# Two modulation units of a trunk step moved ahead of the second output projection, in between the group products

## The reference

```
m = silu(c) @ w_ada + b_ada;  shift, scale, gate = split(m, 3)     # 3 x 1024 values per sublayer
h = x * (1 + scale) + shift
x = layer_norm(ALPHA * x + (1 + gate) * sublayer(h))
```

```
pooled = causal means over windows 2, 4, 8, 16 (one per group of 256 channels) - h
mixed  = einsum('blgc,gcd->blgd', pooled, w_grp) * pool_scale      # 4 groups of 256 x 256
m      = mixed @ w_out
```

## Time and profile before

| | us |
|---|---|
| median of 3 runs (851.91 to 852.33) | 852.32 |
| the profiled execution's own time | 850.87 |
| its span | 849.0 |
| TensorE busy | 741.4 (87%) |
| ScalarE busy | 282.3 (33%) |
| VectorE busy | 240.7 (28%) |
| GpSimd busy | 130.0 (15%) |

### The profile page before, as it was taken

The page is one execution under the profiler, slowest core; times in us unless marked ns, Lnnn a source line. Parts: engine busy times, 40 slices in busy tenths (PEclk is TensorE's granted clock), DMA queues, the critical chain, the costliest instruction groups (busy, mean ns, idle before and its releaser), DMA issues.

```text
span 849.0 us, 22536 instructions
## 1 busy us (share of the span) xinstructions
PE 741.4 (87%) x9606; PEld 463.7 (55%) x9607; DVE 240.7 (28%) x596; ACT 282.3 (33%) x571; POOL 130.0 (15%) x217
## 2 busy tenths in 40 slices
PE   3799999899999999897886789978999979889964
PEld 2378887575655555453443368644555535545532
DVE  1139998714700000000000381272000000000033
ACT  2135677412433333322131250142333223323323
POOL 0170687400001001000000000001101101000101
PEclk9899999799999999999897889999999989999985
DMA  9999523995994989999999999697899999999301
GB/s 313 390 239 359 199 100 119 339 340 201 410 381 192 370 329 405 420 425 426 419 421 417 382 368 407 231 396 308 339 426 415 428 417 426 420 423 424 139 0 51
DMA packets 63885, 280.48 MB, mean 330 GB/s; under 512 B 3013, under 2 KB 3627, under 8 KB 55638
## 3 DMA queue, kind: packets, MB, share of 16 engines
q1 hardware_dynamic: 60738, 271.75, 81.2%
q0 software_dynamic: 2432, 6.94, 2.6%
q10 hardware_dynamic: 676, 1.24, 0.5%
HBM read 277.49 MB, written 3.37 MB: 331 GB/s over the span
## 4 chain that ended last, share of the span: by engine, by line
PE 62%; DMA 21%; DVE 7%; ACT 4%; SPq 2%; issue 2%; POOL 0%; DVEq 0%; ACTq 0%
PE bank L716 17%; DMA ring<-in_w_up 13%; PE bank L850 9%; PE bank L726 7%; PE bank L988 7%; PE bank L689 5%; PE bank L751 4%; DMA big<-in_w_up 4%; DMA ring<-in_w_ada 3%; PE bank L567 3%; DVE t L1353 2%; PE bank L697 2%; ACT big L1291 2%; DMA big<-in_state_pool 2%; SPq L474 1%
## 5 line engine op out<-in xcount | busy, mean ns | idle before, releaser
L716 PE MATMUL bank<-ring,big 128*32 128x256 f32 x2112 | 128.9, 399 | 25.8 <-DMA ring<-in_w_up 22.5
L716 PEld LDWEIGHTS bank<-ring,big 128*32 128x32 f32 x2112 | 70.8, 115 | 79.7 <-DMA ring<-in_w_up 21.1
L1918 POOL TENSOR_TENSOR big<-t 128x192 f32<-128x192 f32 x51 | 26.4, 518 | 547.9 <-PE bank L689 411.7
L1787 DVE SCALAR_TENSOR_TENSOR big<-big,bank 128x128 f32<-128x128 f32 x49 | 17.0, 347 | 307.8 <-ACT big L1289 307.8
L689 PE MATMUL bank<-htm,big 128*32 128x256 f32 x1224 | 75.5, 379 | 1.2 <-POOL big L1921 1.2
L850 PE MATMUL bank<-big,ring 128*128 128x264 f32 x320 | 73.9, 389 | 0.0
L716 PE MATMUL bank<-big 128*32 128x256 f32 x1024 | 63.0, 401 | 9.8 <-DMA big<-in_w_up 6.5
L850 PEld LDWEIGHTS bank<-big,ring 128*128 128x128 f32 x320 | 60.0, 190 | 11.5 <-issue 0.8
L726 PE MATMUL bank<-ring,big 128*32 128x256 f32 x1056 | 63.8, 382 | 0.0
L1289 ACT ACT_TABLE_LOAD x49 | 62.9, 1283 | 1.7 <-issue 0.8
L567 PE MATMUL bank<-ring,cT 128*32 128x256 f32 x768 | 53.6, 426 | 10.2 <-DMA ring<-in_w_ada 9.7
(11 more groups left out here) (252 smaller groups left out, 842.2 us busy)
## 6 DMA issues: line engine op xcount, KB each, us to landing
ring<-in_w_ada SPq DMA_DIRECT2D x24, 2048.0 KB, 18.4
ring<-in_w_gate SPq DMA_DIRECT2D x21, 2048.0 KB, 22.6
ring<-in_w_up SPq DMA_DIRECT2D x21, 2048.0 KB, 24.8
ring<-in_w_down SPq DMA_DIRECT2D x21, 2048.0 KB, 26.5
big<-in_w_gate SPq DMA_DIRECT2D x11, 2048.0 KB, 15.3
big<-in_w_up SPq DMA_DIRECT2D x11, 2048.0 KB, 18.8
big<-in_w_down SPq DMA_DIRECT2D x11, 2048.0 KB, 19.0
ring<-in_w_in_even SPq DMA_DIRECT2D x5, 2048.0 KB, 33.1
```

What stands on the lines that cost most here:

```text
L716: last = mm(GU[C * q:C * (q + 1), :].rearrange("p (a n) -> p a n", a=2), hgc[:, P * (k % 2) + C * (k // 2):P * (k % 2) + C * (k // 2 + 1)] ...
L1918: v.tensor_tensor(flat, all_r, all_b[:, :, bass.ds(g, 1)].broadcast_to([P, 2 * TT, C]), ALU.mult)\
```

## The change

On TensorE, unit 18 with the columns of 17 now stands behind the second group tile, and unit 19, without columns, behind the fourth. The projection has no unit left in it; behind its tiles 1 and 3 only the columns of 18 and of 19 stand. The call of `ada_columns` ahead of the projection is gone, and `ada_unit(20)`, which used to do the columns of 19, finds none pending. On ScalarE the copies of the two units' rows move in the same way between the copies of the group tiles. What is computed is the same.

```diff
@@ -990,8 +990,10 @@
                     last.then_inc(E(name + "_done"), 1)
                     if m == 5:
                         layer_norm_sum(idx, 0)
-                    if m in units:
+                    if units.get(m):
                         ada_unit(units[m])
+                    elif m in units:
+                        ada_columns()
                 layer_norm_sum(idx, 1)
@@ -1045,10 +1047,13 @@
                     last = mm(bank[4 + i % 4][:, 0:T], wgrp[:, g, c, P * hf:P * (hf + 1)], t1[:, 2 * g + c, :],
                               start=(c == 0), stop=(c == 1))
                 last.then_inc(E("grp_done"), 1)
-            ada_columns()
+                if i == 1:
+                    ada_unit(18)
+                if i == 3:
+                    ada_unit(19, False)
             pe.wait_ge(E("prow_copied"), 2)
             pe.wait_ge(E("grp_copied"), 5)
-            projection("out1", 2, t2, 4, lambda i: (E("grp_copied"), i + 1), GROUP_TILES, {3: 18, 5: 19})
+            projection("out1", 2, t2, 4, lambda i: (E("grp_copied"), i + 1), GROUP_TILES, {1: None, 3: None})
             layer_norm_mean(2)
             ada_unit(20)
@@ -1324,8 +1329,8 @@
                 act.wait_ge(E("grp_done"), i + 1)
                 A(fn(t2[:, m, :], bank[4 + i % 4][:, 0:T], ACT.Identity, scale=vec[:, V_PS + m:V_PS + m + 1]),
                   E("grp_copied"))
-            ada_unit(18)
-            ada_unit(19)
+                if i in (1, 3):
+                    ada_unit(18 + i // 2)
             warm_up(ACT.Sqrt)
             layer_norm(2, (20, 21))
             route(1, (22, 23))
```

## The result

The changed kernel takes 858.57 us (median of 7 runs, 855.35 to 859.96) against 852.32 (7 runs, 849.52 to 853.03). The ratio is 1.0065 with a 95% interval of 1.0047 to 1.0083, that is 5.5 us more, 4.0 to 7.1; the two medians by themselves differ by 6.25 us, which is inside that interval. Forecast were 858.1 us and +5.8 us.

What follows compares the result with a forecast made beforehand. Bounds: nearly saturated DMA engines, and TensorE without idle time up to the projection's end. Wait +4.96, lower clock +1.54, old wait -1.31, columns +0.46 and +0.09 gave 5.74 (5.77 step by step), so 858.1 us, range 855.4 to 860.8.

Steps and rivals of the forecast that it cites:

- The wait for unit 18's weights: Behind group tile 1, TensorE arrives at 504.32 and waits until the weights land at 509.28: 4.96 us.
- Unit 18 at the lower clock: After the idle wait, unit 18 takes 3.41 us instead of 1.87, +1.54 us.
- Unit 19 hardly waits, its landing is a floor: Behind group tile 3, TensorE arrives at 514.95, weights land at 514.84; an earlier arrival would wait for that landing.
- the second sum: End of the projection if unit 18 ran at full clock and TensorE waited for unit 19's landing: 5.66 us later.
- The old wait goes: In the group products, waiting and hand-over at VectorE's last pooled pair disappear under the new wait: -1.31 us.
- Columns of 19 win nothing behind the projection: Taking them out of unit 20 gains nothing, as TensorE waits there for ScalarE's squares; 0.46 us saved at most.
- Fills behind the projection's first tile: Layer 1 expert 0's fills go out about 8.8 us later, landing about 540, before use at 580.04 plus the shift: no loss.
- The sum: All terms together: the projection ends 5.77 us later, and what follows moves with it.
- The first (weights there, wait filled): Unit weights are ready in the group products, so the pooling wait is filled: 0.8 us earlier, 851.5 us; 5 in 100.
- The second (absorbed later): DMA waits in the expert loop absorb the later start: no change, 852.3 us; 5 in 100.
- The third (clock stays low): Low clock lasts past unit 18 into later tiles and unit 19: 859.6 us, at the outer end 865.0; 10 in 100.

Runs made afterwards that it cites:

- filled_wait: The changed kernel with ten products on constants ahead of unit 18, inside its wait; 858.10 us, +6.4 us against the kernel before.
- before_again: The kernel before, unchanged, profiled a second time; 34.17 us from the first group product to the last two projection tiles.
- weights_first: The changed kernel with the weight DMAs of units 18 and 19 issued ahead of the projection's two halves; 852.33 us, -0.3 us against the kernel before.
- late_in_groups: The changed kernel with unit 18 moved behind the sixth group tile and unit 19 behind the eighth; 854.69 us, +2.4 us against the kernel before.

## Why the prediction was right, step by step

- *The wait for unit 18's weights.* Forecast 4.96 us. The bracket shows 4.59, counted from the modelled end of the tile ahead; counted from start to start, as the sum does, it is 4.82 (511.08 - 504.46 - 1.80). By the formula it is landing minus arrival; the landing came 1.7 us later in the profile after (510.98 against 509.28), the arrival 1.94. The landings held against their issues, 21.7 and 20.4 us. What the forecast says of a DMA that is busy "nearly throughout" is too much (12 of the 40 slices of the earlier trace rows are below nine tenths), but the sum needs only the stretch of these transfers.
- *Unit 18 at the lower clock.* Forecast 3.41 us, measured 3.45 at a granted clock of 0.53.
- *Unit 19 hardly waits, its landing is a floor.* It started 0.4 us behind its landing. filled_wait turned the slow start into a wait for that landing; its stage is 5.02 us longer than the first of before, where the second sum said 5.66. Unit 19's weights landed 0.7 us earlier in it (494.32 + 20.3, that is 11.6 us behind the first group product instead of 12.3), which is the difference.
- *The old wait goes.* Right in the profile after. But its size, 1.31 us, was that of one execution. In before_again unit 16 and the products behind it ran at a granted clock of 0.50, unit 17 at 0.87, and from unit 16 to the group products were 7.97 us (495.39 to 503.36) instead of 6.54. TensorE reached the last tiles late enough, and there was no wait in the group products at all: they and the columns took 7.79 us, 0.22 more than their 7.57 of work, and the projection began at 511.15 against 511.40. The time that the lower clock cost ahead was given back here. So the term lies between 0.2 and 1.3 us, and the rival that lived on it (the wait filled, 0.8 us) was smaller than I made it.
- *Columns of 19 win nothing behind the projection.* From the norm's product (L606) to the second partial sum of squares (L599) were 4.04 us after (554.68 to 558.72), and 4.03 before (547.03 to 551.06); the columns that no longer stand between them made no difference:

```profile
554.68 0.71 PE L606 MATMUL bank<-ln_part,con 128*128 128x264 f32 x2 [0.51 <-ACT ln_part L1088]
555.33 1.93 PE L567 MATMUL bank<-ring,cT 128*32 128x256 f32 x32
...
558.72 0.65 PE L599 MATMUL bank<-big,con 128*32 128x264 f32 x8 [0.57 <-ACT big L1238]
```

- *Fills behind the projection's first tile.* Expert 0's first fill went out at 526.24, 11.0 us later than before, and landed in 8.2 us instead of 15.3. The queue had run nearly empty just ahead of it (DMA share 0.20 from 525.0 to 526.2), where it was full before (1.05 from 510 to 515):

```profile
526.24 0.34 SPq L474 DMA_DIRECT2D big<-in_w_gate  x1
big<-in_w_gate SPq DMA_DIRECT2D x1, 2048.0 KB, 8.2
525.00:526.20 1.20, 1.20 (x7) 1.04 (x6) 0.00 (x0) 0.00 (x0) 0.00 (x0) 1.00 0.20 79
```

  It was there at 534.4, more than fifty microseconds ahead of its use. Later, and harmless, as forecast; 8.8 us of delay had been forecast, and 1.94 of the 11.0 are the later start of the stage.
- *The sum.* + 5.77 forecast at the end of the projection, + 5.70 measured in the profile, + 5.5 (4.0 to 7.1) in time. Small errors cancel in it: the projection begins 18.02 us behind the first group product instead of 17.90, and the stage from there is 3.44 us shorter than before instead of 3.25, because a set of columns between its tiles costs 0.37 us, not 0.46. That the two sums agree within 0.1 us is in part luck, since the first profile of before happened to have the wait of 1.04 us: against the second the same sum, with 0.22 for 1.31, would have been + 6.9, and + 6.8 and + 6.5 were measured there. The interval in time holds all of these. The mechanism does not hang on it.

The rivals. The first (weights there, wait filled) is refuted by the bracket of 4.59 us; weights_first shows what it would have been worth, half a microsecond won against one profile of before and half a microsecond lost against the other. The second (absorbed later) is refuted by the chain: the fill behind the longest stall moved by 9.37 us with the product that releases it, and the loss is there in the time. The third (clock stays low) did not come: the tiles behind unit 18 took 1.95 us for eight passes (515.00 to 516.95; 1.88 before, 509.15 to 511.03), and unit 19 in 1.87 us. The Trainium skill's account of bursts between DMA waits (TensorE: Matmul & The Clock Gate, "HAM oscillation — how this bites in real kernels") holds here for the wait of 4.59 us and one slow start. In late_in_groups and filled_wait units stand behind waits of 0.75 to 1.23 us and start at the full clock, 1.86 to 1.87 us each (granted clock 1.00), so that not every wait between two bursts brings it.

## What to carry to other kernels

Before work is moved into an idle gap, look up when its inputs land, not only how long it takes: on an in-order engine the moved work turns the gap into a wait for them, and everything queued behind it waits too. With the weight queue saturated, as it was here (DMA share 1.05), moving two fills ahead of two others made them land at 498.7 and 504.1 instead of 509.3 and 514.8 (weights_first against before), so the order of the work and the order of the fills have to be moved together, or the work left where it is. And when two waits stand in a row, removing the first (or the slow clock behind it) may only lengthen the second, as filled_wait shows.

## What the runs showed beyond that

The granted clock of the same piece of work differs from one execution to the next by as much as many a tuning step is worth. The same routing products took 2.97, 4.18, 4.44 and 5.28 us, the same first expert 3.66 or 5.35 us, and one wait of 1.04 us was there in one profile of the kernel before and absent in the other. A stage between two fixed instructions came nearer to the change than the span did: 35.25 and 34.17 against 40.95 and 40.65 us, a difference of 5.4 to 6.8, where the spans differ by 9.0 to 9.8 us (849.0 and 848.3 against 858.1 and 858.0) and the time by 4.0 to 7.1.
